# Attention loop: the last query tile projected at heads 33 to 38 instead of 24 to 31, the longest row's selection rounds spread to head 45

## The chip, the cores and the metric

The kernel runs on one core of a Trainium2 chip. The metric is the device time of one execution in microseconds (us). Five engines work beside each other, each through its own instruction list in order: TensorE (PE, with PEld for its weight loads), VectorE (DVE), ScalarE (ACT), GpSimd (POOL) and SyncE (SP). They wait for each other only where an instruction list has a wait on a semaphore.

## The reference, cut to what matters

Two decoder layers over 512 tokens of width 1024. Each layer projects its modulated input into the queries, keys and values of two head groups; group A is attention over a window of 128 tokens with a sink, group B attends only to the 128 keys that an indexer picks for each query:

```python
def one_block(args):                    # 128 queries of group B
    rel = jax.nn.relu(jnp.einsum('bqhd,bsd->bqhs', qib, ki).astype(jnp.float32))
    score = jnp.einsum('bqhs,bqh->bqs', rel, wb)
    score = jnp.where(causal[None], score, -jnp.inf)
    _, sel = lax.top_k(score, topk)     # topk = 128
    ...
    s = jnp.einsum('bqhgd,bqnhd->bqhgn', qg, ks).astype(jnp.float32) * (D ** -0.5)
    p = jax.nn.softmax(s, axis=-1).astype(v.dtype)
    o = jnp.einsum('bqhgn,bqnhd->bqhgd', p, vs)
```

Both outputs are rms-normalised, joined and projected; layer norm, a SwiGLU block and a second layer norm follow.

## The kernel before

Tokens come in four tiles of 128 (t = 0 to 3). All large products are made three times, on high and low parts of both operands (`split_product`, lines 846 to 848), because the operands are rounded. Weights come in pieces of 128x1024 through a ring of four; each is split into a high half by ACT (line 1628) and a low half by DVE, or by POOL for the first output pieces (line 682).

The attention of a layer is one loop of 64 heads, in eight units of eight: A0, A1, A2, A3 (heads 0 to 31), then B0, B1, B3, B2 (heads 32 to 63). Every engine has its own loop over the same index i, and steps are placed in it by lags and tables of indices. At index i

- PE computes the scores of head i (line 1170; from head 48 on two heads at a time, line 1146), transposes the probabilities of head i-3 (line 1181) and multiplies those of head i-5 by the values (line 1203). The scores wait until DVE has masked head i-2, or i-3 where three banks rotate (from `QB_FREE` on); the transposes wait for ACT's exponential. After each unit its output is transposed (line 1211), and DVE and ACT split it.
- DVE adds the mask and takes the maximum (`mask_scores`, line 2288). ACT takes the exponential (line 1718) and copies the transposed probabilities (line 1727). Behind each unit DVE normalises (lines 2314 to 2321), ACT squares (1737), POOL takes the root (646), ACT scales (1744), and the high and low halves of the transposed output follow (ACT 1751, DVE 2338).

Two more jobs ride in the same loop. The first is the projection of group B's queries, four tiles of four steps. A step (`project_qb`) is one weight piece on one tile: two `split_product`, six matmuls of 128x512 into bank 5. `QB_STEPS` gives the head index of every step; the first three run ahead of the loop. When a tile is done, ACT copies it out (line 1667, one index later), POOL rotates it (lines 576, 577, 582, at `ROPE_AT`, two indices later), PE transposes it (line 1106, at `QB_AT`) and ACT copies the transposes (1694). Tile 3 is needed by unit B3, from head 48 on. Bank 5 is also used to reduce a modulation vector in the first layer (line 868, at `REDUCE_AT`; DVE takes it two indices later, line 2148) and, from head `QB_FREE` on, as a third bank for scores.

The second is the indexer's choice of 128 keys. Sixteen rounds on each of three rows (t = 3: 512 wide, t = 2: 384, t = 1: 256) each take the eight largest (`top_max`, line 2241) and strike them out (`top_replace`, line 2249). Two rounds of each row come ahead of the loop, three more of the longest; `ROUNDS_AT` places the others. `top_mask` (line 2266) then turns a row into a mask, at `MASKS_AT`; it is needed by the first head of its unit. In DVE's loop a head's maxima stand ahead of its mask and the replacements behind it.

On POOL, `GAIN_AT` places the scaling of the output weights (line 674) and `WO_AT` their low halves.

Of the kernel before, what the change touches and what calls it, by code (L numbers as in the profile page):

```python
# [20 lines left out]
TOPK = min(256, SEQ // 4)  # L21
# [5 lines left out]
T = SEQ // P  # L27
# [10 lines left out]
CP = tuple(KD // k for k in CK)  # L38
# [25 lines left out]
def own_units(n):  # L64

    units = [("G1", 0), ("X", 0)]
    for f in range(n):
# [15 lines left out]
P_RING = 4  # L83
QB_BANK = 5

QB_FREE = 40
REDUCE_AT = 36
PAIRS_FROM = 48
PT_RING = 4
DVE_HEADS = (3, 7)  # L90
# [3 lines left out]


QB_FRONT = 3
QB_STEPS = (None,) * QB_FRONT + (1,) + tuple(4 + 5 * n // 2 for n in range((T - 1) * CP[4]))
ROPE_AT = tuple(QB_STEPS[CP[4] * t + CP[4] - 1] + 2 for t in range(T))
QB_AT = (9, 21, 30, 45)

# [8 lines left out]
EARLY_ROUNDS = 2  # L109
INDEX_ROUNDS = 3  # L110
ROUNDS_AT = {1: [5 * n // 2 for n in range(TOPK // 8 - EARLY_ROUNDS)],
             2: [8, 12, 16, 19, 24, 26, 29] + [39, 41, 43, 46, 48, 50, 52],
             3: [1 + 13 * n // 4 for n in range(TOPK // 8 - EARLY_ROUNDS - INDEX_ROUNDS)]}
ROUND_TILES = {i: [t for t in IDX_TILES if i in ROUNDS_AT[t]] for i in range(64)}
MASKS_AT = {36: (1,), 41: (3,), 54: (2,)}


SH1, SC1, SH2, SC2, GT1, GT2 = range(6)
# [19 lines left out]
def build_trunk(nc, x, x_t, c_col, positions, inv_freq, weights, w_ada, b_ada, b_gate, ln_col, ln_row, sinks, g_col, out):  # L138
    with ExitStack() as ctx:
# [311 lines left out]
        def at_evac(l, c, t):  # L451

            return at_chunk(l, c, t) - T
# [4 lines left out]
        def at_head(l, u, h):  # L458
            return 64 * l + 8 * u + h + 1
# [76 lines left out]
        def s_bank(n):  # L536

            return bank[3 + n % 2] if n < QB_FREE else bank[(QB_BANK, 3, 4)[(n - QB_FREE) % 3]]

# [296 lines left out]
        def _(pe):  # L836
# [312 lines left out]
            def head_scores(l, u, h):  # L1149
# [7 lines left out]
                else:  # L1157

                    pe.wait_ge(masked, at_head(l, u, h) - (2 if n < QB_FREE else 3))
                if n == QB_FREE:  # L1160
                    pe.wait_ge(proj_evac, at_evac(l, 4, T - 1))
# [11 lines left out]
            def transpose_p(l, u, h):  # L1173
                lo, hi = keys_of(UNITS[u])
                pe.wait_ge(probs, at_head(l, u, h))
                if before := back(u, h, 2):

                    wait_pT(pe, l, *before)
                n = 8 * u + h
                for b in range((hi - lo) // P):  # L1180
                    m = pe.transpose(bank[6 + h % 2][:, b * P:(b + 1) * P],  # L1181
                                     prob[:, n % P_RING, b * P:(b + 1) * P], ident[:])
                m.then_inc(p_transposed, 1)
# [74 lines left out]
            def attention(l):  # L1258
                in_bank2 = ("chunk", 3)
                for i in range(64 + LAG_Y):  # L1260
                    if i == REDUCE_AT and l == 0:

# [6 lines left out]
                    if 0 <= i - LAG_T < 64:  # L1269
                        transpose_p(l, (i - LAG_T) // 8, (i - LAG_T) % 8)  # L1270
                    if i in QB_STEPS:
                        project_qb(l, QB_STEPS.index(i) // CP[4], QB_STEPS.index(i) % CP[4])
                    if 0 <= i - LAG_V < 64:
# [341 lines left out]
        def _(act):  # L1615
# [114 lines left out]
            def sink_weight(l, u):  # L1730
                act.wait_ge(sink_diff, 4 * l + u + 1)
                nc.scalar.activation(es[:, u % 2, :], es[:, u % 2, :], ACT.Exp).then_inc(sink_exp, 1)
# [21 lines left out]
            def attention(l):  # L1754
                for i in range(64 + LAG_SPLIT):
# [4 lines left out]
                    if i < 64:  # L1760
                        exponential(l, i // 8, i % 8)
                        u, h = i // 8, i % 8
                        if h == 7 and UNITS[u][0] == "A":
                            sink_weight(l, u)
                    if i - 1 in QB_STEPS[CP[4] - 1::CP[4]]:
                        evacuate(l, 4, QB_STEPS.index(i - 1) // CP[4])
                    for lag, part in ((LAG_NORM, square_y), (LAG_SCALE, scale_y), (LAG_SPLIT, split_y)):
# [303 lines left out]
        def _(dve):  # L2071
# [405 lines left out]
            def attention(l):  # L2477
                for i in range(64 + LAG_SPLIT):
                    for t in ROUND_TILES.get(i, ()):
                        top_max(t)  # L2480
                    if i == REDUCE_AT + 2 and l == 0:
                        take_mod(2, QB_BANK)
# [5 lines left out]
                    for t in ROUND_TILES.get(i, ()):  # L2488
                        top_replace(t)
                    for t in MASKS_AT.get(i, ()):  # L2490
                        top_mask(t)
# [515 lines left out]
```

## Time and profile before

| | |
|---|---|
| median of 3 runs | 1244.72 us (1244.66 to 1244.84) |
| profiled execution | 1244.9 us, span from first to last instruction 1243.2 us, granted TensorE clock 0.998 |
| PE busy | 1208.3 us (97% of the span) |
| DVE, ACT, POOL busy | 945.8, 594.5, 359.7 us (76%, 48%, 29%) |
| attention loop, first layer | heads 0 to 63 from 125.9 to about 229.5 us |
| attention loop, second layer | from about 735 to 836.6 us |

The profile names an instruction by line, engine, operation and the tiles it writes and reads. "Busy" is the time in which an engine had an instruction at work; an entry in square brackets is the idle time ahead of an instruction and what ended it. PE's and DVE's instructions overlap a little at their ends, so the distance between two starts is what one costs in a row of them.

### The profile page before, as it was taken

The page shows a single profiled execution, that of the slowest core. Times are in us where ns is not written, and L with a number is a line of the kernel's source. Part 1 is how long each engine was busy: PE and PEld are TensorE (multiplying, and loading weights), DVE is VectorE, ACT ScalarE, POOL GpSimd, SP SyncE. Part 2 cuts the span into 40 slices and gives each one's busy share as a digit, 9 for nine tenths or more (in the row PEclk, how much of TensorE's full clock was granted, in tenths as well). Part 3 has the DMA queues.
Part 4 walks back from the last instruction along what each step waited for, and adds up shares of the span by engine and source line. Part 5 has one row for each costly group of instructions (what it writes and reads, how often), then busy time and mean ns, then how long its engine had stood idle before and what let it go on. Part 6 is the DMA issues. An engine that isn't in the chain of part 4 may idle for free. (4 is left out here: it accounts for less than half of the span.)

```text
span 1243.2 us, 20784 instructions
## 1 busy us (share of the span) xinstructions
PE 1208.3 (97%) x7354; PEld 1056.4 (85%) x7354; DVE 945.8 (76%) x1634; ACT 594.5 (48%) x1206; POOL 359.7 (29%) x345
## 2 busy tenths in 40 slices
PE   6999999999999999999999999999999999999997
PEld 5778887889888889999888688778989998899986
DVE  6899987777788795777876599858796776377648
ACT  3655668345333233555144566871545552255520
POOL 4237337600121001221117367581012200122200
PEclk9999999999999999999999999999999999999999
DMA  9872201434888422334833220114223333133331
GB/s 357 323 267 88 86 15 55 135 119 138 279 283 268 148 85 85 105 112 150 296 91 113 69 69 2 35 52 170 85 77 98 115 119 104 60 115 110 119 107 68
DMA packets 45452, 160.75 MB, mean 129 GB/s; under 512 B 5936, under 2 KB 5936, under 8 KB 45360
## 3 DMA queue, kind: packets, MB, share of 16 engines
q1 hardware_dynamic: 30528, 109.07, 26.9%
q0 software_dynamic: 13536, 49.29, 11.7%
q10 hardware_dynamic: 1296, 1.17, 0.3%
q8 instruction: 57, 0.93, 0.3%
q14 instruction: 35, 0.29, 0.1%
HBM read 157.41 MB, written 2.10 MB: 128 GB/s over the span
## 5 line engine op out<-in xcount | busy, mean ns | idle before, releaser
L1628 ACT ACTIVATE w_hi<-w_raw 128x1024 fp32r<-128x1024 f32 x104 | 108.4, 1060 | 152.5 <-PE bank L848 140.2
L846 PE MATMUL bank<-w_hi,hT_hi 128*128 128x512 f32 (+2 forms) x392 | 148.1, 378 | 3.5 <-ACT pq L1667 2.0
L2090 DVE TENSOR_TENSOR w_lo<-w_raw,w_hi 128x1024 fp32r<-128x1024 f32 x96 | 123.7, 1303 | 28.4 <-ACT w_hi L1628 27.0
L848 PE MATMUL bank<-w_hi,hT_lo 128*128 128x512 f32 (+2 forms) x392 | 142.6, 364 | 0.0
L847 PE MATMUL bank<-w_lo,hT_hi 128*128 128x512 f32 (+2 forms) x392 | 142.5, 363 | 0.0
L715 POOL TENSOR_TENSOR w_raw<-ada_w,w_raw 128x512 f32<-128x512 f32 x28 | 37.1, 1325 | 363.2 <-DVE w_lo L2648 200.7
L1312 PE MATMUL bank<-hT_lo,w_hi 128*128 128x256 f32 x448 | 112.3, 283 | 0.0
L1310 PE MATMUL bank<-hT_hi,w_hi 128*128 128x256 f32 x448 | 112.3, 283 | 0.0
L846 PE MATMUL bank<-w_hi,gu_hi 128*128 128x512 f32 x264 | 102.9, 390 | 0.0
L848 PE MATMUL bank<-w_hi,gu_lo 128*128 128x512 f32 x264 | 102.7, 389 | 0.0
L847 PE MATMUL bank<-w_lo,gu_hi 128*128 128x512 f32 x264 | 102.7, 389 | 0.0
L846 PEld LDWEIGHTS bank<-w_hi,hT_hi 128*128 128x128 f32 x392 | 73.9, 188 | 22.4 <-issue 7.0
L1312 PEld LDWEIGHTS bank<-hT_lo,w_hi 128*128 128x128 f32 x448 | 86.0, 192 | 0.1
L1310 PEld LDWEIGHTS bank<-hT_hi,w_hi 128*128 128x128 f32 x448 | 86.0, 192 | 0.1
L2655 DVE TENSOR_TENSOR w_lo<-w_raw,w_hi 128x1024 fp32r<-128x1024 f32 x28 | 34.3, 1225 | 65.2 <-POOL ada_w L720 54.8
L848 PEld LDWEIGHTS bank<-w_hi,hT_lo 128*128 128x128 f32 x392 | 73.9, 188 | 11.6
L847 PEld LDWEIGHTS bank<-w_lo,hT_hi 128*128 128x128 f32 x392 | 74.0, 189 | 9.9 <-issue 0.5
L1718 ACT ACTIVATE pq<-pq,nmax 128x256 f32<-128x256 f32 (+3 forms) x128 | 66.7, 521 | 30.4 <-DVE nmax L2288 29.8
L646 POOL TENSOR_TENSOR rs_out<-rs_in,minus_half 128x1 f32<-128x1 f32 x31 | 21.4, 690 | 201.8 <-DVE rs_in L2365 160.7
L846 PE MATMUL bank<-hT_hi,w_hi 128*128 128x512 f32 x192 | 75.1, 391 | 0.0
L848 PE MATMUL bank<-hT_hi,w_lo 128*128 128x512 f32 x192 | 74.8, 389 | 0.0
L847 PE MATMUL bank<-hT_lo,w_hi 128*128 128x512 f32 x192 | 74.7, 389 | 0.0
(308 smaller groups left out, 3266.7 us busy)
## 6 DMA issues: line engine op xcount, KB each, us to landing
w_raw<-in_weights SPq DMA_DIRECT2D x184, 512.0 KB, 3.6
ada_w<-in_w_ada POOLq DMA_DIRECT2D x76, 512.0 KB, 5.3
ada_w<-in_w_ada SPq DMA_DIRECT2D x4, 512.0 KB, 6.7
qT<-in_w_ada SPq DMA_DIRECT2D x4, 512.0 KB, 10.3
xs<-in_x_t SPq DMA_DIRECT2D x4, 512.0 KB, 16.3
xs<-in_x POOLq DMA_DIRECT2D x4, 512.0 KB, 6.8
g_row<-in_ln_row POOLq DMA_DIRECT2D x4, 512.0 KB, 6.0
b_row<-in_ln_row POOLq DMA_DIRECT2D x4, 512.0 KB, 6.9
```

The source lines that it names most:

```text
L646: nc.gpsimd.tensor_tensor(rs_out[:, n:n + 1], rs_in[:, n:n + 1], minus_half[:], ALU.pow)\
L715: nc.gpsimd.tensor_tensor(gate[:, 0:HALF], x_row[:, HALF:PW], gate[:, 0:HALF], ALU.subtract)\
L846: pe.matmul(dst, a_hi, b_hi, start=first, stop=False)
L847: pe.matmul(dst, a_hi, b_lo, start=False, stop=False)
L848: return pe.matmul(dst, a_lo, b_hi, start=False, stop=last)
L1310: pe.matmul(dst, w, m_hi[:, k, :], start=first and k == 0, stop=False, skip_group_check=not first)
L1312: pe.matmul(dst, w, m_lo[:, k, :], start=False, stop=False, skip_group_check=not first)
L1628: nc.scalar.activation(w_hi[:, p % RING, :], w_raw[:, p % RING, :], ACT.Copy).then_inc(hi_ready, 1)
L1718: nc.scalar.activation(p, p, ACT.Exp, scale=-1.0, bias=nmax[:, u % 2, h:h + 1], accum_out=rowsum[:, u % 2, h:h + 1]).then_inc(probs, 1)
L2090: nc.vector.tensor_tensor(w_lo[:, p % RING, :], w_raw[:, p % RING, :], w_hi[:, p % RING, :].bitcast(F32), ALU.subtract).then_inc(lo_ready, 1)
L2655: nc.vector.tensor_tensor(both_in(w_lo, r, "S2", f), w_raw[:, slot(r.l, gate_piece(r, f)), :], both_in(w_hi, r, "S2", f).bitcast(F32), ALU ...
```

## The change

Two single indices and three tables of indices change, and a new table names the steps of the last tile. No instruction is added or taken away; where rows differ in number, neighbours are counted together differently.

```diff
-QB_FREE = 40
-REDUCE_AT = 36
+QB_FREE = 44
+REDUCE_AT = 41
@@
-QB_STEPS = (None,) * QB_FRONT + (1,) + tuple(4 + 5 * n // 2 for n in range((T - 1) * CP[4]))
+QB_LAST = (33, 35, 37, 38)
+QB_STEPS = (None,) * QB_FRONT + (1,) + tuple(4 + 5 * n // 2 for n in range((T - 2) * CP[4])) + QB_LAST
@@
-             3: [1 + 13 * n // 4 for n in range(TOPK // 8 - EARLY_ROUNDS - INDEX_ROUNDS)]}
+             3: [1 + 22 * n // 5 for n in range(TOPK // 8 - EARLY_ROUNDS - INDEX_ROUNDS)]}
@@
-MASKS_AT = {36: (1,), 41: (3,), 54: (2,)}
+MASKS_AT = {36: (1,), 46: (3,), 54: (2,)}
```

The steps of tile 3 were at heads 24, 26, 29 and 31 and are at 33, 35, 37 and 38. Through `ROPE_AT`, POOL's rotation of tile 3 goes from index 33 to 40. The eleven rounds of the 512-wide row were at heads 1, 4, 7, 10, 14, 17, 20, 23, 27, 30, 33 and are at 1, 5, 9, 14, 18, 23, 27, 31, 36, 40, 45. Since a line is added near the top, every line number behind it is one higher in the changed kernel.

PE at head 33, the second head of unit B0 (scores, transposes of head 30, values of head 28, scores of head 34), before:

```order
L1170 MATMUL bank4<-kT,qT 128x128
L1181 MATMUL bank6<-ident,pq 128x128 x2
L1203 MATMUL bank1<-v_a,pT 128x128 x2
L1170 MATMUL bank3<-kT,qT 128x128
L1181 MATMUL bank7<-ident,pq 128x128 x2
```

and in the changed kernel:

```order
L1171 MATMUL bank4<-kT,qT 128x128
L1182 MATMUL bank6<-ident,pq 128x128 x2
L847 MATMUL bank5<-w_hi,hT_hi 128x512
L848 MATMUL bank5<-w_lo,hT_hi 128x512
L849 MATMUL bank5<-w_hi,hT_lo 128x512
L847 MATMUL bank5<-w_hi,hT_hi 128x512
L848 MATMUL bank5<-w_lo,hT_hi 128x512
L849 MATMUL bank5<-w_hi,hT_lo 128x512
L1204 MATMUL bank1<-v_a,pT 128x128 x2
```

The six matmuls of one projection step have come between the transposes and the values; they stood in the same place of head 24.

DVE at heads 40 and 41, the first of unit B1 (`ISA pq,nmax` is the masked maximum), before:

```order
L2288 ISA pq,nmax<-bank5,scores 128x256
L2288 ISA nmax 128x1
L2241 MAX top8<-scores 128x8
L2288 ISA pq,nmax<-bank3,scores 128x256
L2288 ISA nmax 128x1
L2249 MATCH_REPLACE scores<-top8,scores 128x384
L2266 TENSOR_SCALAR scores<-scores 128x512
```

and in the changed kernel:

```order
L2242 MAX top8<-scores 128x8
L2289 ISA pq,nmax<-bank3,scores 128x256
L2289 ISA nmax 128x1
L2250 MATCH_REPLACE scores<-top8,scores 128x512
L2242 MAX top8<-scores 128x8
L2289 ISA pq,nmax<-bank4,scores 128x256
L2289 ISA nmax 128x1
L2250 MATCH_REPLACE scores<-top8,scores 128x384
```

A round of the 512-wide row now surrounds the mask of head 40, the row's `top_mask` (line 2266) has gone from here, and the scores of these two heads come in banks 3 and 4.

POOL from the root of unit 2 on, before:

```order
L646 TENSOR_TENSOR rs_out<-rs_in,minus_half 128x1
L576 TENSOR_TENSOR scratch<-pq,sin_t 128x512
L577 TENSOR_TENSOR scratch<-pq,cos_t 128x512
L582 TENSOR_TENSOR pq<-scratch 128x512
L795 DMA scratch<-in_b_gate 128x1024
L646 TENSOR_TENSOR rs_out<-rs_in,minus_half 128x1
L674 TENSOR_SCALAR w_raw<-w_raw,gcol 128x512 x2
L682 TENSOR_TENSOR w_lo<-w_raw,w_hi 128x1024
```

and in the changed kernel:

```order
L647 TENSOR_TENSOR rs_out<-rs_in,minus_half 128x1 x2
L675 TENSOR_SCALAR w_raw<-w_raw,gcol 128x512 x2
L577 TENSOR_TENSOR scratch<-pq,sin_t 128x512
L578 TENSOR_TENSOR scratch<-pq,cos_t 128x512
L583 TENSOR_TENSOR pq<-scratch 128x512
L796 DMA scratch<-in_b_gate 128x1024
L683 TENSOR_TENSOR w_lo<-w_raw,w_hi 128x1024
```

The rotation of tile 3 and the DMA of the gate row behind it have moved from ahead of the root of unit 3 and the first gain to behind them.

## Rows read from the trace of the kernel before

**Rows 1.** Windows: start:end, length, busy (x instructions) of each engine, clock, DMA.

```profile
core 0: us, PE busy (x) PEld busy (x) DVE busy (x) ACT busy (x) POOL busy (x), PEclk, DMA share, GB/s
161.06:177.03 15.97, 15.50 (x99) 13.34 (x98) 14.58 (x52) 10.89 (x36) 4.74 (x5) 1.00 0.01 2
177.03:196.47 19.44, 17.49 (x134) 15.39 (x133) 14.69 (x62) 15.99 (x57) 13.02 (x11) 1.00 0.15 43
...
784.58:803.59 19.01, 16.01 (x119) 13.69 (x117) 14.96 (x61) 15.82 (x57) 13.03 (x11) 1.00 0.13 43
```

**Rows 2.** PE in time, head 24: start, duration, instruction, [idle ahead, its releaser].

```profile
162.35 0.50 PE L846 MATMUL bank<-w_hi,hT_hi 128*128 128x512 f32 x1 [0.47 <-ACT pq L1667]
...
164.28 0.60 PE L1170 MATMUL bank<-kT,qT 128*128 128x256 f32 x2
```

**Rows 3.** DVE in time, first layer, start of head 24 and heads 28 to 30.

```profile
162.77 0.55 DVE L2241 MAX8 top<-scores 128x8 f32<-128x384 f32 x1
...
171.20 0.48 DVE L2288 CUSTOM_DVE_ANT_0 pq<-bank,band,nsink 128x256 f32<-128x256 f32 x1
...
171.60 0.56 DVE L2241 MAX8 top<-scores 128x8 f32<-128x384 f32 x1
172.07 0.47 DVE L2288 CUSTOM_DVE_ANT_0 pq<-bank,band,nsink 128x256 f32<-128x256 f32 x1
...
173.00 0.16 DVE L2314 TENSOR_TENSOR es<-rowsum,es 128x8 f32<-128x8 f32 x1
...
174.04 1.01 DVE L2241 MAX8 top<-scores 128x8 f32<-128x512 f32 x2
174.97 0.47 DVE L2288 CUSTOM_DVE_ANT_0 pq<-bank,band,nsink 128x256 f32<-128x256 f32 x1
...
176.42 0.15 DVE L2330 TENSOR_SCALAR rs_in<-mean_sq 128x1 f32<-128x1 f32 x1
```

**Rows 4.** PE in time, first layer: heads 33, the reduction, 39 and 48.

```profile
177.91 0.39 PE L1170 MATMUL bank<-kT,qT 128*128 128x128 f32 x2
...
180.91 1.84 PE L868 MATMUL bank<-ones,ada_acc 128*128 128x1 f32 x16
...
184.58 0.39 PE L1170 MATMUL bank<-kT,qT 128*128 128x128 f32 x2
...
196.47 1.13 PE L1146 MATMUL bank<-kT,qT 64*128 64x512 f32 x4
```

**Rows 5.** PE in time, second layer: head 38, transposes of head 45, scores of 48.

```profile
790.40 0.49 PE L1170 MATMUL bank<-kT,qT 128*128 128x128 f32 x2 [0.44 <-DVE nmax L2288]
...
800.76 0.63 PE L1106 MATMUL bank<-ident,pq 128*128 128x128 f32 x4 [0.84 <-DVE hT_lo L2338]
...
803.59 1.13 PE L1146 MATMUL bank<-kT,qT 64*128 64x512 f32 x4
```

**Rows 6.** DVE and ACT in time: mask of head 42 in both layers, normalisation, square.

```profile
189.52 0.42 DVE L2288 CUSTOM_DVE_ANT_0 pq<-bank,scores 128x256 f32<-128x256 f32 x1
...
796.63 0.42 DVE L2288 CUSTOM_DVE_ANT_0 pq<-bank,scores 128x256 f32<-128x256 f32 x1
...
801.45 0.69 DVE L2321 TENSOR_TENSOR pk<-bank,recip 128x512 f32<-128x512 f32 x1
...
802.25 0.59 ACT L1737 ACTIVATE bank<-pk 128x512 f32<-128x512 f32 x1
```

**Rows 7.** POOL and DVE in time, first layer: rotation, gain, low half, two column masks.

```profile
179.53 1.28 POOL L576 TENSOR_TENSOR scratch<-pq,sin_t 128x512 f32<-128x512 f32 x1 [2.33 <-ACT pq L1667]
...
186.93 3.12 POOL L674 TENSOR_SCALAR w_raw<-w_raw,gcol 128x512 f32<-128x512 f32 x2
...
207.74 2.36 POOL L682 TENSOR_TENSOR w_lo<-w_raw,w_hi 128x1024 fp32r<-128x1024 f32 x1 [2.71 <-ACT w_hi L1628]
...
189.07 0.41 DVE L2266 TENSOR_SCALAR scores<-scores 128x512 f32<-128x512 f32 x1
...
208.29 2.02 DVE L2266 TENSOR_SCALAR scores<-scores 128x384 f32<-128x384 f32 x1
```

## The prediction, made before the changed kernel was run

> **What bounds the kernel now.** A new order of the same work can only win where TensorE (PE) idles, so I read the busy times of the attention loop first, the only part that is reordered (64 heads in each layer) [rows 1]. Heads 24 to 31 last 15.97 us; PE is busy in 15.50 and VectorE (DVE) in 14.58, so PE sets the pace and DVE is close behind. Heads 32 to 47 last 19.44 us in the first layer and 19.01 in the second, with PE busy in 17.49 and 16.01: some 2 and 3 us of bubbles. That, with a wait at head 24, is the whole prize. The order of time of PE then says where the bubbles of the second layer lie: from head 38 on, 0.44 us for DVE's masked scores at head 38, 0.84 for DVE's low half ahead of the transposes of the last query tile [rows 5]. The scores of head 48 come at 196.47 and 803.59 us [rows 4, 5]; from there PE is nearly always busy, so what shifts them shifts the end.
>
> All steps below are on the first layer's clock. Head 32 starts 607.55 us later in the second layer (784.58 against 177.03 [rows 1]), and I subtract that.
>
> **Part 1: four projection blocks leave heads 24 to 31.** Head 24 lasts from 161.06 [rows 1] to 164.28 [rows 2], 3.22 us; a head without a block takes 1.10. A block of six products adds about 1.40, and 0.72 is the wait for ACT's (ScalarE's) copy of the tile before, shown as 0.47 idle [rows 2]. So 4 x 1.40 + 0.72 = 6.3 us leave, and PE alone would need 9.65 us for the eight heads.
>
> DVE does not let it, because the scores of head n wait until the mask of head n-2 is done. DVE's steps, start to start [rows 3]: a 256-wide mask 0.40; a selection round on the 384-wide row 0.47 for the maximum and 0.53 for the replacement, 1.00 together; the 512 and 256 rows together 0.93 + 1.05, which I split by length into 1.26 and 0.73; the normalisation 1.04. In heads 24 to 31 the new order has 8 masks (3.2), 3 rounds of 256 (2.2), 3 of 384 (3.0), still 2 of 512 (2.5; heads 27 and 31 for 27 and 30), the normalisation, a low half of 0.6 with 0.2 of wait, and 0.3 of small ones: 13.0 us. DVE starts head 24 at 162.77 [rows 3]; with the round of head 20 gone I take 162.25, not the whole 1.26 earlier, since it then waits for scores. So head 31 is through at 175.3, and its mask, for which head 33 waits, is done at 174.45. Head 33 started at 177.91 [rows 4]. **Of 6.3 us removed, 3.4 arrive at head 33**; the rest becomes PE idle, in heads 29 to 33.
>
> **Part 2: the blocks come back at heads 33, 35, 37 and 38.** They cost 4 x 1.40 = 5.6 us on PE, on the path, since there was no bubble before head 38. They replace the wait of head 38 in the second layer (0.44), and in the first the reduction of 1.84 us [rows 4], which moves from head 36 to 41. With the intervals of before plus the blocks, from 174.45: head 38 at 183.0, head 39 at 185.0. Before, head 38 of the second layer was at 182.85 [rows 5], head 39 of the first at 184.58 [rows 4].
>
> **Part 3: heads 39 to 47, where DVE and ACT set the pace.** The change puts two 512 rounds here (heads 40 and 45), and the PE blocks are over by then. DVE cannot use the slow heads 33 to 38 to get ahead, since it waits for their scores. From head 39 on: mask at 185.5, round done 186.25; head 40 with the 512 row and a 0.34 mask until 187.85; head 41 until 189.2; the mask of head 42 ends at 189.55. Before, it ended at 189.87 in the first layer and 189.43 in the second [rows 6]. From there to the scores of head 48 the chain was 6.6 us in both layers ([rows 4, 5] less those two): exponential, ACT's conversion of a weight piece, high half, low half, masks, normalisation, ACT's square, ACT's copy of the queries. The 512 round of head 45 falls into it. ACT's square began at 802.25, 0.2 after the product of the normalisation (801.45, 0.6 to the next) was there [rows 6]; apart from that the round adds to the chain, 1.15 us.
>
> Second layer: 189.55 + 6.6 + 1.15 = 197.3 against 196.04, **+1.3 us**.
>
> First layer: the reduction now stands ahead of the scores of head 41 and waits for ACT's copy of the last tile, which follows the exponential of head 39. It starts at about 186.8 and ends at 188.6; DVE gets the scores of head 41 some 0.9 late, and head 42 is masked at 190.4. 190.4 + 6.6 + 1.15 = 198.15 against 196.47, **+1.7 us**.
>
> **GpSimd (POOL).** The rotation of the last query tile, three operations of 1.28 us [rows 7], moves behind the root of unit 3 and the gain of 3.12. Asked for at 184.7, the root, gain and rotation end at 192.5; the transposes of head 45 wait for DVE's low half until 193.1 or later. That cover is 0.6 us. Behind the rotation are queued the gate row's DMA, the low half of the first output piece, the next gain and the root of unit 4, which ends at about 199.5; ACT wants it at 198.7 in the second layer, ahead of a conversion and the copy on which PE waits at head 50. I take **+0.2 us**. SyncE's piece loads hang on POOL's low halves; no PE wait of the loop is for them, and a slip of 2 us is no longer than the head shift.
>
> **Parts at nothing.** The 512-wide column mask moves from head 41 to 46, 0.41 us either way. Two score banks instead of three for heads 40 to 43: DVE's pace hides it; uncovered, a few tenths. The two 512 rounds that leave heads 0 to 23 gave DVE's time only, where PE set the pace.
>
> **The sum**: 1.3 + 1.7 + 0.2 = +3.2 us. The profiled execution took 1244.9 us (span 1243.2, 1.7 around it), the median of the runs is 1244.72; so **1247.9 us**.
>
> **Rivals.**
> - *The bubbles are filled.* PE runs without a gap through heads 33 to 47, DVE and ACT having caught up. By busy times: 17.49 + 5.6 - 19.44 - 3.4 = +0.25 in the first layer, 16.01 + 5.6 - 19.01 - 3.4 = -0.8 in the second: 1244.2. For it: the room in [rows 1]. Against: the blocks end at head 38, where the bubbles begin. 20%.
> - *Faster.* DVE keeps up in heads 24 to 31 as well; all 6.3 us arrive, up to 2 x 2.9 less than the last case, 1238.4, and 1241.3 with half. It decides once DVE does those heads in under 11.5 us. Against it: the 13.0 above is DVE's own work. 7%.
> - *POOL last.* If root, gain and rotation slip by more than the 0.6 us of cover, or ACT waits longer for the root of unit 4, each further microsecond counts: about 1 us in each layer, 1250. 8%.
> - *The column mask of head 46 meets POOL.* The 384-wide one took 2.02 us and ended 0.2 after POOL's low half of 207.74; the 512-wide one took 0.41 although POOL was in its gain from 186.93 on [rows 7]. At head 46, about 197.2, the gain runs (195.8 to 198.9), so I take no wait; were the low half there, 1.5 us a layer, 1250.9. 5%. The Trainium skill (SBUF — State Buffer, "SBUF: two separate sides") has an exclusive lock there, with the second to start waiting for any GpSimd operation. By that page the gain would hold the mask too; the 0.41 speaks against it.
> - *The forecast*, +1.5 to +4.5: 60%.
>
> **Chances.** About 0.2%, 2.5 us, is what a measurement of this kernel tells from no change, and the forecast lies just past it. Slower by more: 0.42 of the forecast's 0.60, with POOL's 0.08 and the mask's 0.05, 0.55. Within: 0.18 and the filled bubbles' 0.20, 0.38. Faster: 0.07. The range, from just under the filled bubbles to the mask case: 1243.6 to 1250.9.
>
> **What would show it.** Right: heads 24 to 31 about 12.5 to 13 us long, with PE waiting for DVE's masks for some 3 us; no PE idle in heads 34 to 38; the gaps of heads 40 to 47 still there and wider; the scores of head 48 1.3 and 1.7 us later in their layers; heads 48 on unchanged at 33.0 us. Wrong: heads 24 to 31 at 10 us (DVE was not close), heads 40 to 47 without gaps (a lead did carry), or PE waiting for POOL's rotation at head 45.

## The result and the profile after

The changed kernel takes **1251.31 us** (median of six runs, 1250.95 to 1251.48) against 1244.74 us for the kernel before in the same session: a ratio of 1.0051, 95% interval 1.0040 to 1.0062. It is slower by 6.6 us. The profiled execution spans 1249.4 us against 1243.2. The direction was forecast, the size was not: +3.2 us was, and the measured time lies 0.4 us above the end of the range.

The loop of 64 heads can be cut where its scores start. This table holds the lengths of five stretches in us, first layer / second layer, from the starts of the score matmuls in PE's order of time. From head 48 on PE computes the scores of two heads at a time, so head 60 is the seventh of these pairs:

| stretch | before | changed | difference | forecast |
|---|---|---|---|---|
| head 0 to 24 | 35.17 / 34.94 | 35.16 / 34.94 | 0.0 / 0.0 | 0 |
| head 24 to 33 | 16.85 / 16.87 | 14.21 / 14.21 | -2.64 / -2.66 | -3.46 |
| head 33 to 39 | 6.67 / 5.99 | 10.54 / 10.53 | +3.87 / +4.54 | +3.88 / +4.56 |
| head 39 to 48 | 11.89 / 12.13 | 13.33 / 12.24 | +1.44 / +0.11 | +1.26 / +0.17 |
| head 48 to 60 | 21.48 / 21.48 | 21.87 / 22.41 | +0.39 / +0.93 | +0.2 once |

That is +3.05 and +2.92 us. Another +0.28 stands ahead of head 0 of the first layer, where nothing was changed; in the other kernels below this offset lies between -0.20 and +0.50, so I count it to no edit. The three make 6.25 us, and the span grew by 6.2. The 0.4 us between that and the 6.6 of the medians is in no trace: the profiled execution was 0.2 us above its median before and 0.2 below it in the changed kernel.

The busy times of the same stretches up to head 48, as in [rows 1], of the changed kernel (start:end, length, busy time of each engine, clock, DMA):

```profile
core 0: us, PE busy (x) PEld busy (x) DVE busy (x) ACT busy (x) POOL busy (x), PEclk, DMA share, GB/s
161.33:175.54 14.21, 11.82 (x82) 10.05 (x80) 13.98 (x49) 9.64 (x33) 4.35 (x5) 1.00 0.01 2
175.54:186.08 10.54, 10.54 (x69) 9.50 (x70) 6.92 (x30) 7.27 (x29) 0.30 (x1) 1.00 0.00 1
186.08:199.41 13.33, 11.19 (x83) 9.88 (x81) 10.61 (x39) 9.40 (x29) 12.93 (x10) 1.00 0.25 74
...
771.88:786.09 14.21, 11.81 (x82) 10.05 (x81) 13.98 (x49) 9.64 (x33) 9.31 (x9) 1.00 0.01 2
786.09:796.62 10.53, 10.53 (x68) 9.50 (x69) 6.91 (x30) 7.27 (x29) 0.29 (x1) 1.00 0.01 2
796.62:808.86 12.24, 9.85 (x67) 8.03 (x65) 10.35 (x38) 9.29 (x29) 11.84 (x10) 1.00 0.17 52
```

In heads 24 to 32 the two engines have changed places: DVE is busy in 13.98 of 14.21 us and PE in 11.8, where PE was busy in 15.50 of the 15.97 us of heads 24 to 31 before [rows 1]. In heads 33 to 38 PE is busy without a gap and DVE has 3.6 us to spare. What PE waited for in the attention loop of the first layer, in the changed kernel (engine, line, what it waited for: us, times, longest):

```profile
PE bank L1171 <- DVE nmax L2289: 3.1, 6, 0.9
PE bank L1147 <- ACT qT L1695: 1.2, 1, 1.2
PE bank L1107 <- DVE hT_lo L2339: 0.7, 1, 0.7
```

The first line is the masks that PE now waits for, the second the copy of the queries ahead of head 48, where PE did not wait before. In order of time PE's places are these (they answer to [rows 4] and [rows 5]):

```profile
175.54 0.49 PE L1171 MATMUL bank<-kT,qT 128*128 128x128 f32 x2 [0.20 <-DVE nmax L2289]
...
187.86 1.95 PE L869 MATMUL bank<-ones,ada_acc 128*128 128x1 f32 x16 [0.30 <-ACT pq L1668]
...
195.39 0.63 PE L1107 MATMUL bank<-ident,pq 128*128 128x128 f32 x4 [0.65 <-DVE hT_lo L2339]
...
199.41 1.13 PE L1147 MATMUL bank<-kT,qT 64*128 64x512 f32 x4 [1.19 <-ACT qT L1695]
...
808.86 1.13 PE L1147 MATMUL bank<-kT,qT 64*128 64x512 f32 x4 [1.19 <-ACT qT L1695]
```

Two places explain most of what the forecast lacks. The first is at the end of head 23. VectorE's difference of unit 2, on operands of 128x8, takes 1.00 us where it took 0.17, with GpSimd's rotation of the third query tile started 0.3 us ahead of it (DVE, then POOL, in the changed kernel):

```profile
161.75 1.00 DVE L2304 TENSOR_TENSOR es<-nmax,nsink 128x8 f32<-128x8 f32 x1
162.67 0.08 DVE L2250 MATCH_VALUE_LOAD scores<-top,scores 128x8 f32 x1
...
161.45 1.27 POOL L577 TENSOR_TENSOR scratch<-pq,sin_t 128x512 f32<-128x512 f32 x1
```

The difference ends at 162.75, GpSimd's first product at 162.72. The second layer has the same row, 1.00 us at 772.29. Before, the difference came first:

```profile
162.02 0.17 DVE L2303 TENSOR_TENSOR es<-nmax,nsink 128x8 f32<-128x8 f32 x1
...
162.38 1.30 POOL L576 TENSOR_TENSOR scratch<-pq,sin_t 128x512 f32<-128x512 f32 x1 [0.75 <-ACT pq L1667]
```

The second place is GpSimd's order of time in the second layer, from the root of unit 3 on, with the step of ScalarE that waits for its end:

```profile
796.33 0.55 POOL L647 TENSOR_TENSOR rs_out<-rs_in,minus_half 128x1 f32<-128x1 f32 x1 [10.65 <-DVE rs_in L2331]
796.86 3.12 POOL L675 TENSOR_SCALAR w_raw<-w_raw,gcol 128x512 f32<-128x512 f32 x2
799.96 1.27 POOL L577 TENSOR_TENSOR scratch<-pq,sin_t 128x512 f32<-128x512 f32 x1
...
804.76 2.38 POOL L683 TENSOR_TENSOR w_lo<-w_raw,w_hi 128x1024 fp32r<-128x1024 f32 x1
807.12 3.36 POOL L675 TENSOR_SCALAR w_raw<-w_raw,gcol 128x512 f32<-128x512 f32 x2
810.45 0.57 POOL L647 TENSOR_TENSOR rs_out<-rs_in,minus_half 128x1 f32<-128x1 f32 x1
...
811.05 0.72 ACT L1745 ACTIVATE pk<-pk,rs_out 128x512 f32<-128x512 f32 x1 [0.70 <-POOL rs_out L647]
```

After 10.65 us of idle time GpSimd works through 14.7 us without a real gap, and the root of unit 4 is its last piece. ScalarE stands for 0.70 us, with a conversion of 1.04 us and the next heads' copies and exponentials behind the wait.

A smaller third is the column mask of head 46, which now stands beside the scores of head 48. In the first layer it began in the last 0.4 us of GpSimd's gain and took 0.69 us (DVE, then POOL), in the second 0.42 (808.72):

```profile
199.27 0.69 DVE L2267 TENSOR_SCALAR scores<-scores 128x512 f32<-128x512 f32 x1
...
196.57 3.11 POOL L675 TENSOR_SCALAR w_raw<-w_raw,gcol 128x512 f32<-128x512 f32 x2
```

### The profile page after: what moved, and what is told of

It reads as the page before. It is cut to its first block and busy times, and to the rows that moved or that the text cites. A ratio compares the mean times of both kernels' runs of the same rounds, so it can differ in the third digit from the quotient of the medians.

```text
span 1249.4 us, 20787 instructions
## 1 busy us (share of the span) xinstructions
PE 1209.8 (97%) x7354; PEld 1057.9 (85%) x7354; DVE 946.8 (76%) x1634; ACT 595.9 (48%) x1206; POOL 359.9 (29%) x345
## 3 DMA queue, kind: packets, MB, share of 16 engines
q10 hardware_dynamic: 1296, 1.17, 0.3%
```

## The experiments

The table gives the lengths of the stretches for every kernel (first / second layer, us) and the sum of each layer against before; the text below each expectation says what follows. The profiled executions of one kernel and the next agree to 0.1 us wherever nothing was changed, so a few tenths can be read in a stretch though not in a total. Some of the expectations count a pair of heads behind head 48 as one: their "head 51" and "head 54" are heads 54 and 60, and their "root of unit 5" is the root of unit 4, which ScalarE waits for behind head 48.

| kernel | 24 to 33 | 33 to 39 | 39 to 48 | 48 to 60 | layers against before | median us |
|---|---|---|---|---|---|---|
| before | 16.85 / 16.87 | 6.67 / 5.99 | 11.89 / 12.13 | 21.48 / 21.48 | | 1244.7 to 1244.9 |
| changed | 14.21 / 14.21 | 10.54 / 10.53 | 13.33 / 12.24 | 21.87 / 22.41 | +3.05 / +2.92 | 1251.31 |
| rounds only | 16.11 / 16.12 | 6.76 / 6.72 | 14.10 / 14.10 | 21.61 / 21.61 | +1.68 / +2.08 | 1248.49 |
| blocks only | 14.60 / 14.57 | 10.53 / 10.53 | 12.60 / 11.17 | 21.48 / 22.70 | +2.26 / +2.50 | 1250.19 |
| copy late | 13.39 / 13.82 | 10.53 / 10.53 | 13.32 / 12.23 | 21.85 / 22.42 | +2.19 / +2.50 | 1250.02 |
| rounds by 38 | 14.22 / 14.22 | 10.53 / 10.53 | 13.68 / 10.61 | 21.48 / 24.38 | +3.00 / +3.26 | 1251.07 |
| gain first | 14.22 / 14.22 | 10.53 / 10.53 | 14.28 / 12.23 | 21.60 / 21.60 | +3.64 / +2.15 | 1250.26 |
| root before gain | 14.22 / 14.22 | 10.52 / 10.53 | 13.33 / 12.23 | 22.35 / 22.36 | +3.50 / +2.88 | 1251.59 |
| root and round | 14.22 / 14.22 | 10.53 / 10.53 | 13.28 / 11.19 | 22.31 / 22.31 | +3.40 / +1.80 | 1250.01 |
| three mended | 13.39 / 13.81 | 10.52 / 10.52 | 12.28 / 10.41 | 21.48 / 22.62 | +0.72 / +0.88 | 1246.92 |
| four mended | 13.38 / 13.80 | 10.53 / 10.52 | 12.27 / 10.40 | 21.92 / 21.92 | +1.17 / +0.18 | 1246.76 |
| blocks 2 and 2 | 13.79 / 13.87 | 8.44 / 8.84 | 13.35 / 13.35 | 21.48 / 21.49 | +0.06 / +1.06 | 1247.97 |
| blocks 3 and 1 | 14.77 / 14.79 | 6.72 / 6.72 | 15.87 / 15.81 | 21.48 / 21.13 | +1.86 / +2.02 | 1249.30 |
| first block at 25 | 16.26 / 16.24 | 6.67 / 5.59 | 11.89 / 12.01 | 21.49 / 21.49 | -0.66 / -1.14 | 1243.04 |

### Each half of the change alone

Rounds only, an edit of the kernel before:

```diff
-             3: [1 + 13 * n // 4 for n in range(TOPK // 8 - EARLY_ROUNDS - INDEX_ROUNDS)]}
-MASKS_AT = {36: (1,), 41: (3,), 54: (2,)}
+             3: [1 + 22 * n // 5 for n in range(TOPK // 8 - EARLY_ROUNDS - INDEX_ROUNDS)]}
+MASKS_AT = {36: (1,), 46: (3,), 54: (2,)}
```

> The kernel before with the second half of the change alone: the longest row's selection rounds at heads 1, 5, 9, 14, ... 36, 40, 45 and its column mask at head 46; the projection blocks stay at heads 24 to 31. My theory: the 512-wide round of head 45 (a maximum of 0.69 and a replacement of 0.68, 1.2 us start to start) stands on the chain from the mask of head 42 to the scores of head 48, and the root of unit 5 is asked for later by the same step, so ScalarE waits for it ahead of head 50. Head 48 about 1.2 us later in each layer, its wait on ScalarE's copy of the queries there as in the changed kernel (1.19), another 0.3 to 0.9 by head 51: +2.5 to +3.5 us in all, 1247.2 to 1248.2. Rival, the rounds cost only together with the blocks (DVE gets to head 45 late because of them): within 1 us of the kernel before, no wait at head 48.

Measured: 1248.49 us, ratio 1.0029 (1.0019 to 1.0040). The wait of 1.19 us ahead of head 48 is there in both layers, as the theory has it, and the rival falls. Behind head 48 only 0.13 us are lost, less than the 0.3 to 0.9 that I expected, and ScalarE's wait for the root does not show. Heads 39 to 47 cost 2.2 and 2.0 us more, not 1.2, since the round of head 40 is paid here too; heads 24 to 32 give 0.75 back. Head 25 starts 2.49 us after head 24 in the first layer, 3.22 before: the wait of the first block for ScalarE's copy has gone.

Blocks only, the changed kernel with these two lines put back (`13 * n // 4`, mask at 41).

> The changed kernel with the rounds and the column mask of the longest row back where they were (heads 1, 4, 7, ... 30, 33; mask at head 41); the last tile's blocks stay at heads 33, 35, 37, 38 and the reduction at head 41. My theory: heads 24 to 32 as in the changed kernel (14.2 us instead of 16.9), heads 33 to 38 too, then heads 39 to 47 without the two 512-wide rounds: head 48 1.2 to 1.8 us earlier than in the changed kernel in each layer, so +1.2 in the first layer and 0 to +0.5 in the second against before, and no wait for the root of unit 5. In all about +2 us with the collision of the es difference in it (0.8 us a layer): 1246 to 1248. If the two halves add up, this one and the run with the rounds alone together make the 6.6 us of the whole; rival, each half alone costs little (under 1 us) and only both together meet.

Measured: 1250.19 us, ratio 1.0042 (1.0025 to 1.0059), 2.2 us above the top of what I expected. The halves give +3.6 and +5.3 us, together 8.8 against the 6.6 of the whole, so they don't add up. Behind the blocks the two late rounds cost less than in the kernel before: the stretch from head 39 to 48 is 0.7 and 1.1 us longer in the changed kernel than with the blocks alone. And in the second layer blocks only loses 1.22 us after head 48, where I had expected nothing: ScalarE waits 1.11 us for the root of unit 4. The root is ready at 809.92, whatever VectorE has gained by then. The second layer's column mask also met the rotation there, 1.30 us at 799.17.

### The small difference under the rotation

Copy late, an edit of the changed kernel in ScalarE's loop:

```diff
-                    if i - 1 in QB_STEPS[CP[4] - 1::CP[4]]:
-                        evacuate(l, 4, QB_STEPS.index(i - 1) // CP[4])
+                    for t in [t for t in range(T) if i == QB_STEPS[CP[4] * t + CP[4] - 1] + (2 if t == 2 else 1)]:
+                        evacuate(l, 4, t)
```

> The changed kernel with ScalarE's copy of the third query tile one place later, behind the sink weight of head 23, so that GpSimd's rotation of that tile can't begin before VectorE's 128x8 difference of unit 2 is through (1.00 us in the changed kernel, 0.17 in the kernel before). My theory: the difference takes 0.17 again in both layers, and since VectorE sets the pace of heads 24 to 33 the 0.83 arrive at head 33 and at the end: -1.7 us, 1249.6. Rival: the 0.83 are absorbed (PE's idle time at head 26 shrinks, and that of heads 29 to 33 grows): head 33 within 0.2 of the changed kernel, 1251.3.

Measured: 1250.02 us, 1.3 less than the changed kernel. Its rows in DVE's and POOL's order of time, first layer and then second:

```profile
161.90 0.17 DVE L2304 TENSOR_TENSOR es<-nmax,nsink 128x8 f32<-128x8 f32 x1
...
163.16 1.28 POOL L577 TENSOR_TENSOR scratch<-pq,sin_t 128x512 f32<-128x512 f32 x1 [1.66 <-ACT pq L1668]
...
781.23 0.59 DVE L2315 TENSOR_TENSOR es<-rowsum,es 128x8 f32<-128x8 f32 x1
...
779.30 2.50 POOL L697 TENSOR_TENSOR xs<-xs,b_row 128x512 f32<-128x512 f32 x2
```

In the first layer the difference takes 0.17 us, head 33 comes 0.82 sooner, and 0.86 stand at the end: shown. In the second layer the difference takes 0.17 us too, but only 0.4 arrive, so the total falls 0.4 short of the theory. The rotation has moved on to its next collision: GpSimd's row operations behind it now end at 781.80, and VectorE's sum of unit 2, again 128x8, takes 0.59 us until 781.82 (0.15 in the changed kernel).

The Trainium skill (SBUF — State Buffer, "SBUF: two separate sides") has for this that a VectorE instruction with two SBUF inputs and a GpSimd instruction that reads SBUF exclude each other for their whole length. The trace agrees: both stalls end with GpSimd's instruction, within 0.03 us. The prediction cites this section for the column mask and does not apply it to the differences.

### The late rounds, and what stood behind them

Rounds by 38, an edit of the changed kernel:

```diff
-             3: [1 + 22 * n // 5 for n in range(TOPK // 8 - EARLY_ROUNDS - INDEX_ROUNDS)]}
-MASKS_AT = {36: (1,), 46: (3,), 54: (2,)}
+             3: [1, 5, 9, 14, 18, 23, 27, 31, 34, 36, 38]}
+MASKS_AT = {36: (1,), 41: (3,), 54: (2,)}
```

> The changed kernel with the last three rounds of the longest row at heads 34, 36 and 38 instead of 36, 40 and 45, and its column mask at head 41 instead of 46: the same rounds, but in the stretch where PE runs the blocks and VectorE waits for scores (0.85 to 1.05 us idle a head). My theory: nothing is paid at heads 34 to 38; VectorE has 1.2 us less at head 40 and 1.2 less at head 45, so head 48 comes 1.2 to 2 us earlier in each layer, ScalarE's 1.19 wait there is gone, and the wait for the root of unit 5 behind it: -3 to -5 us, 1246.5 to 1248.5. Rival: ScalarE or PE's own work sets heads 39 to 48 and the rounds are beside it: at most -1 us, 1250.3 to 1251.3.

Measured: 1251.07 us, nothing gained: the totals fit the rival, the stretches do not. The rounds of heads 34 and 36 indeed cost nothing (33 to 39 stays 10.53), and in the second layer head 48 comes 1.63 us sooner, without its wait. Then all of it is lost, here on ScalarE and PE:

```profile
811.25 0.72 ACT L1745 ACTIVATE pk<-pk,rs_out 128x512 f32<-128x512 f32 x1 [2.99 <-POOL rs_out L647]
...
813.33 0.41 PE L1182 MATMUL bank<-ident,pq 128*128 128x128 f32 x2 [2.57 <-ACT pT L1728]
```

ScalarE stands for 2.99 us until GpSimd's root, which comes at the same time as in the changed kernel (811.0 there, 811.2 here). So there are two limits one behind the other. GpSimd's rotation is late as well: PE waits 1.09 us for it ahead of the transposes of the last tile (804.30). In the first layer two other things stand where the gain should be. The column mask of head 41 met the rotation (DVE, then POOL), and the granted clock fell:

```profile
191.29 1.35 DVE L2267 TENSOR_SCALAR scores<-scores 128x512 f32<-128x512 f32 x1
...
191.09 1.26 POOL L578 TENSOR_TENSOR scratch<-pq,cos_t 128x512 f32<-128x512 f32 x1
...
190.00:194.00 4.00, 4.00 (x19) 3.45 (x18) 3.47 (x10) 2.01 (x7) 3.69 (x3) 0.61 0.00 0
```

### GpSimd's chain

Gain first, one number in the changed kernel:

```diff
-GAIN_AT = (39, 44, 49, 54, 58, 60, 62, 64)
+GAIN_AT = (37, 44, 49, 54, 58, 60, 62, 64)
```

> The changed kernel with GpSimd's first gain (3.12 us) one place ahead of the root of unit 3 instead of behind it, in the 10.6 us in which GpSimd is idle there in the second layer. The trace of the changed kernel has a chain on GpSimd in the second layer: root of unit 3 at 796.33, gain, rotation of the last tile, the gate row's transfer, low half, second gain, root of unit 4 until 811.0, without a gap; ScalarE waits 0.70 for that root, and in the run with the rounds by head 38 it waits 2.99. My theory: this chain is a second limit just behind that of VectorE; with the gain ahead the whole of it comes 3 us earlier, ScalarE's wait is gone, and head 51 stands 0.7 us earlier in the second layer, 0 to 0.3 in the first: -0.7 to -1.2 us, 1250.1 to 1250.6. Rival: the 0.70 are absorbed by PE's own work in heads 48 to 51: no change, 1251.3.

Measured: 1250.26 us, 1.05 less. In the second layer ScalarE no longer waits for the root, and the stretch behind head 48 is 21.60 us instead of 22.41, nearly the 21.48 of before. That confirms the second limit. The first layer does not answer this question: heads 39 to 48 took 0.95 us more there, most likely because the granted clock was 0.60 from 190 to 192 us and 0.55 from 192 to 194.

Root before gain, the other way to the same end:

```diff
-GAIN_AT = (39, 44, 49, 54, 58, 60, 62, 64)
-WO_AT = (42, 47, 52, 57)
+GAIN_AT = (39, 46, 50, 54, 58, 60, 62, 64)
+WO_AT = (42, 49, 52, 57)
```

> The changed kernel with GpSimd's root of unit 4 ahead of the second gain instead of behind it, and the second low half and its conversion on ScalarE two heads later (49 instead of 47). The heads up to 48 stay as they are. Theory: the stretch from head 48 to head 54, 21.87 and 22.41 us in the changed kernel (first and second layer) against 21.48 in both before, grew because ScalarE waits for that root (0.70 us idle in the second layer) with the probabilities of heads 46 and 47 queued behind the wait; with the root first the stretch is 21.5 again in both layers: -0.4 and -0.9, 1250.0 us. Rival: the growth comes from VectorE (its low half waits 2.40 and 2.96 us for ScalarE's high half there, 2.03 before) and stays, or ScalarE's conversion, now nearer the low half, costs as much at head 52: no change, 1251.3.

Measured: 1251.59 us, no gain: my rival was right. From head 48, head 52 comes 0.65 us sooner in the second layer, but PE then waits 0.63 instead of 0.48 for VectorE's mask at head 54, and the second conversion waits for the gain (0.20) and stands closer to ScalarE's high half. Between heads 54 and 56 another 0.4 us go in both layers. The low half that was moved back pushes GpSimd's third gain back, ScalarE's third conversion waits for that, and PE for the copy behind it (second layer):

```profile
820.31 1.06 ACT L1629 ACTIVATE w_hi<-w_raw 128x1024 fp32r<-128x1024 f32 x1 [0.33 <-POOL w_raw L675]
...
822.00 0.63 PE L1182 MATMUL bank<-ident,pq 128*128 128x128 f32 x4 [0.20 <-ACT pT L1728]
```

The stretch is 22.36 us in the second layer and, worse, 22.35 in the first. The second conversion alone does not hold head 54: in four mended, below, it stands in the same place, no column mask stands at head 46, and head 54 comes 9.37 us after head 48, as before (9.81 here).

Root and round is that kernel with the row's last rounds at heads 36, 38 and 40:

```diff
-             3: [1 + 22 * n // 5 for n in range(TOPK // 8 - EARLY_ROUNDS - INDEX_ROUNDS)]}
+             3: [1, 5, 9, 14, 18, 23, 27, 31, 36, 38, 40]}
```

> The run with the root ahead of the gain, and the longest row's last three rounds at heads 36, 38 and 40 instead of 36, 40 and 45; its column mask stays at head 46. Against that run it prices one 512-wide round on the chain ahead of head 48, with GpSimd's limit out of the way. Theory: head 48 comes 1.0 to 1.2 us sooner in each layer (the prediction's 1.15), ScalarE's 1.19 us wait there is gone, and the gain stays to the end: -2.0 to -2.4 us against the run before it. Rival: the round stood beside the wait for ScalarE's low and high halves: under 0.5 us a layer, -1 us or less in all.

Measured: 1250.01 us, 1.6 less than the run before it and 0.4 short of the theory. The scores of head 48 in the second layer, of root before gain and of this one:

```profile
809.37 1.13 PE L1147 MATMUL bank<-kT,qT 64*128 64x512 f32 x4 [1.19 <-ACT qT L1695]
```

```profile
807.82 1.13 PE L1147 MATMUL bank<-kT,qT 64*128 64x512 f32 x4
```

From head 39 to 48 the second layer takes 11.19 us instead of 12.23, and the 1.04 us last to head 60. That is the price of the round of head 45; the prediction had 1.15. In the first layer 13.28 us stand against 13.33: the granted clock was 0.66 from 190 to 195 us, which most likely hides it.

### All of it mended, and other places for the blocks

Three mended joins copy late, gain first and the rounds by head 38, with the column mask at head 39.

```diff
-GAIN_AT = (39, 44, 49, 54, 58, 60, 62, 64)
+GAIN_AT = (37, 44, 49, 54, 58, 60, 62, 64)
-MASKS_AT = {36: (1,), 46: (3,), 54: (2,)}
+MASKS_AT = {36: (1,), 39: (3,), 54: (2,)}
```

> The changed kernel with three things mended at once: ScalarE's copy of the third tile behind the sink weight (as in the run with the late copy), the last rounds of the longest row at heads 34, 36 and 38 with its mask at head 39 (ahead of GpSimd's rotation, which made that mask 1.35 us instead of 0.41 in the first layer), and the first gain ahead of the root of unit 3. My theory: 0.8 a layer from the copy, 0.9 to 1.6 at head 48 from the rounds, and from head 48 to the end 33.0 us as in the kernel before, since the root of unit 4 is no longer late. Head 48 at 70.3 to 71 us from head 0 in the first layer and 69.3 to 69.8 in the second: about the kernel before, 1244 to 1246. It would show that the whole loss was three collisions and not the blocks. Rival: the blocks in heads 33 to 38 cost in themselves (nothing of DVE's or ACT's idle time there comes back): at least +2 us stay, 1247 or more.

Measured: 1246.92 us, ratio 1.0018 (1.0009 to 1.0028), so 4.4 of the 6.6 us are back. Head 48 stands at 69.67 us from head 0 in the second layer, 0.26 ahead of before; in the first at 71.30, 0.3 beyond what I expected. The second layer then gives 1.14 away behind head 48: ScalarE waits 1.03 for the root again, since VectorE has moved ahead of GpSimd once more.

Four mended adds the order of root before gain to it (`GAIN_AT = (37, 46, 50, ...`, `WO_AT = (42, 49, ...`).

> The run with three things mended, with the root of unit 4 ahead of the second gain as well. There ScalarE waited 1.03 us for that root in the second layer and head 48 to 54 took 22.62 us against 21.48 before. Theory: that stretch is 21.5 again: -1.1 us in the second layer, nothing in the first (21.48 already), so about 1 us above the kernel before in all, 1245.5 to 1246. The blocks in heads 33 to 38 would then cost under 1 us, and the rest of the loss was what stood around them. Rival: another limit takes the root's place (VectorE's masks of 512): no change, 1246.9.

Measured: 1246.76 us, ratio 1.0015 (1.0006 to 1.0024): in the second layer 0.70 less and only 0.18 above before, in the first 0.45 more. The 0.45 are those between heads 54 and 56 again: ScalarE's third conversion waits 0.34 us for the gain in both layers. The total fits the rival, the second layer the theory but for 0.4.

Blocks 2 and 2, and blocks 3 and 1, edits of three mended:

```diff
-QB_LAST = (33, 35, 37, 38)
+QB_LAST = (27, 30, 34, 37)
```

> The run with three things mended, and the last tile's blocks at heads 27, 30, 34 and 37 instead of 33, 35, 37 and 38. In the changed kernel PE idles 2.2 to 2.6 us in heads 24 to 32, where VectorE sets the pace, and PE sets the pace in heads 33 to 38. My theory: two blocks of 1.40 stand in the idle time of heads 24 to 32 for nothing or nearly so, and two are gone from the path: -1.5 to -2.8 us a layer against the run with four blocks behind, so below the kernel before by 1 to 4 us: 1241 to 1244. Rival: a block delays the scores that VectorE waits for next, so PE's and VectorE's times add up rather than overlap: within 1 us of the run with three things mended.

Measured: 1247.97 us (1245.81 to 1248.62), no faster than three mended. Its ten executions fall apart: three took 1245.8 to 1245.9 us, seven 1247.6 to 1248.6, at a mean granted clock of 0.995 to 0.998. The profiled one is of the first kind, so the stretches tell of 1245.9 us, 1 us below three mended's trace; what the others lose, and where, no trace shows. Two blocks among heads 24 to 32 cost only 0.40 and 0.06 us: there my theory holds. The two that are gone from heads 33 to 38 give 2.1 and 1.7 us back. But heads 39 to 47 grow by 1.1 and 2.9, with PE waiting 0.28 and 1.02 us for masks at heads 39 and 40: VectorE has the rounds of heads 36 and 38 and the column mask (1.06 us under the rotation at 794.88) to do and no PE blocks to do them beside.

> As the run with two blocks in each stretch, but with the blocks at heads 26, 29, 31 and 36. By busy times PE would have 9.65 + 4.2 = 13.9 us of work in heads 24 to 32 and VectorE 10.5 to 12.2, so PE sets the pace there again and the third block is paid there instead of behind. My theory: within 0.7 us of the run with the blocks two and two, on either side. Rival, if the copy of the last tile and GpSimd's chain behind it still set heads 44 to 48: 1 to 3 us faster than that run, since the copy comes sooner.

Here `QB_LAST` is (26, 29, 31, 36). Measured: 1249.30 us, 1.3 above the two and two, where I had allowed 0.7. The third block costs 1.0 us in heads 24 to 32, as the busy times said. The rest lies in heads 39 to 47: with the last block at head 36 the rotation falls ahead of the root of unit 3, ScalarE waits 3.04 us for that in both layers, and the granted clock fell in both. How much each costs was not separated (second layer: ACT, PE, and the windows of that place):

```profile
798.58 0.72 ACT L1745 ACTIVATE pk<-pk,rs_out 128x512 f32<-128x512 f32 x1 [3.04 <-POOL rs_out L647]
...
799.61 0.30 PE L1182 MATMUL bank<-ident,pq 128*128 128x128 f32 x1 [2.51 <-ACT pT L1728]
...
796.00:800.00 4.00, 1.19 (x7) 0.72 (x7) 2.49 (x10) 1.42 (x5) 2.22 (x3) 1.00 0.33 114
800.00:804.00 4.00, 4.00 (x20) 3.39 (x19) 1.48 (x5) 3.75 (x12) 1.66 (x1) 0.59 0.06 19
```

### A version that beats both

First block at 25, an edit of the kernel before and nothing else. It puts the first two blocks of the last tile one head later each, at heads 25 and 27:

```diff
-QB_STEPS = (None,) * QB_FRONT + (1,) + tuple(4 + 5 * n // 2 for n in range((T - 1) * CP[4]))
+QB_STEPS = (None,) * QB_FRONT + (1,) + tuple(4 + 5 * n // 2 for n in range((T - 2) * CP[4])) + (25, 27, 29, 31)
```

> The kernel before with the four blocks of the last tile at heads 25, 27, 29 and 31 instead of 24, 26, 29 and 31; nothing else moves. In the kernel before the first block waits at head 24 for ScalarE's copy of the tile before it (0.47 us idle, 0.72 over the plain head), and in the run with the rounds alone moved that wait was gone and heads 24 to 32 took 16.1 us instead of 16.9. Theory: with the block one head later the copy is there, and PE, which sets the pace in these heads, gains 0.5 to 0.7 us a layer: -1.0 to -1.4 us, 1243.3 to 1243.7, a small gain over the kernel before. Rival: VectorE, busy for 14.6 of these 16 us, becomes the limit at heads 26 to 31 and the gain is under 0.2 us a layer: within 0.4 us of the kernel before.

Measured: **1243.04 us** (1242.90 to 1243.44), ratio 0.9986 (0.9977 to 0.9995): 1.8 us below the kernel before, a bit more than expected, and 8.3 below the changed one. The stretch from head 24 to 33:

```profile
160.83:177.09 16.26, 16.26 (x106) 14.10 (x105) 15.32 (x57) 12.58 (x41) 4.92 (x5) 1.00 0.01 2
767.77:784.01 16.24, 16.24 (x107) 14.12 (x105) 15.30 (x57) 12.56 (x40) 9.93 (x9) 1.00 0.01 2
```

PE has no gap left here, 0.6 us a layer gained. In the second layer another 0.5 comes between heads 33 and 48, where PE's second wait for a mask, at head 39 (0.24 us), is gone. There the 256-wide column mask had stood under GpSimd's last product of the rotation (before, and this kernel):

```profile
790.26 0.81 DVE L2266 TENSOR_SCALAR scores<-scores 128x256 f32<-128x256 f32 x1
...
788.80 0.30 DVE L2266 TENSOR_SCALAR scores<-scores 128x256 f32<-128x256 f32 x1
```

## Why the prediction was right in direction and wrong in size

**Right:**
- *Part 1's mechanism.* Heads 24 to 31 last 12.76 us (12.5 to 13 forecast), with VectorE as the limit and 2.4 us of waits for its masks up to head 33 (about 3 forecast).
- *Part 2.* Head 33 to 39 takes 10.54 and 10.53 us, with PE busy throughout; 10.55 was forecast.
- *Part 3.* Head 39 to 48 takes 13.33 and 12.24 us, against 13.15 and 12.3. The reduction starts 1.78 us after head 39 (1.8 forecast). The round of head 45 costs 1.04 (1.15).
- *The filled bubbles* did not come: PE is busy in 11.19 of 13.33 us and 9.85 of 12.24 there.

**Wrong:**
- *Part 1, the start of VectorE's sum.* "With the round of head 20 gone I take 162.25": the first maximum of head 24 came at 163.34. Of the 1.1 us, 0.27 is the offset ahead of the loop and 0.83 the difference held by the rotation. The 13.0 us of work behind it were right, so the whole slip arrived: -2.64 instead of -3.46, in both layers, 1.6 us in all. I had counted what VectorE does and not where GpSimd would then be. Before, the difference starts at 162.02 and the rotation at 162.38, 0.36 us behind it. In the changed kernel the difference is 0.27 us sooner, ScalarE's copy 0.91 (160.80 instead of 161.71), and so the rotation stands ahead: 0.17 us became 1.00. Copy late shows it, 0.86 us in the first layer, and in the second 0.4 because another small sum takes its turn.
- *POOL's +0.2 us and "heads 48 on unchanged".* From head 48 to 60 the layers grew by 0.39 and 0.93 us, 1.1 more than I gave them. The mechanism was written down (the root behind the second gain, ScalarE waiting ahead of a conversion), and as a rival with about 1 us a layer and a chance of 8%. I had the root end at 199.5 where ScalarE wants it at 198.7 in the second layer, and still took 0.2 for these 0.8 us, as if PE had that much to spare. In fact the wait was 0.70 and arrived. The whole chain hangs on the root of unit 3, which the change delays by slowing heads 33 to 38. Gain first gives 0.8 of the second layer's 0.93 back.
- *The column mask at nothing.* "0.41 us either way" is wrong at head 46, from where VectorE carries it to PE's wait for a mask at head 54 (0.47 us in the first layer, 0.20 before). The stretch from head 48 to 60 is 21.48 us where neither that mask nor a wait for the root stands (first layer of blocks only, rounds by 38 and three mended), 21.60 or 21.61 where the mask takes 0.42 (rounds only, gain first), 21.85 and 21.87 where it takes 0.66 and 0.69 (first layer of copy late and of the changed kernel). So the mask is the first layer's 0.39, and the 0.12 of the second that gain first leaves.
- The last 0.28 us is the offset that belongs to no edit.

So 1.6 + 1.1 + 0.3 is 3.0 of the 3.1 us between +3.2 and the 6.25 of the span. The column mask's own rival came in small: 0.27 us in the first layer instead of 1.5 in each, since it met the end of the gain and not the low half. The same mask took 1.35, 1.30 and 1.06 us in kernels where it met GpSimd's products.

As for the change itself: the blocks can stand in heads 33 to 38 for little. With what stood around them mended, the second layer is within 0.2 us of before and the first 1.2 above. But in none of the eleven orders tried here did moving the blocks out of these heads win anything over the kernel before; that no order could is not shown.

## What to carry to other kernels

Where one engine's lead is used up by the next, add up the other engines' chains to the end as well, each from the event that it really starts from: here a repair on VectorE of 1.6 us gave nothing until GpSimd's chain was shortened too. When a change moves two engines against each other in time, list the short operations that used to pass between the long ones. And before moving a whole group of work, try to move only its first members past the wait that they meet: two blocks one head later each won 1.8 us, the whole group seven to nine heads later lost 6.6.

## What the runs showed of the hardware

- A VectorE operation on 128x8 elements with both inputs in SBUF took 1.00 us instead of 0.17 while a GpSimd product of 128x512 ran, and 0.59 instead of 0.15 in another kernel; it ended with GpSimd's instruction each time. Such a wait shows as a longer instruction and not as idle time at a semaphore; the opening of this text, where engines wait only at semaphores, leaves it out.
- A column mask (one input, 128x512) took 0.41 us beside GpSimd's gain (one input) in the kernel before [rows 7] and 1.35 us beside its product of two inputs (rounds by 38). Beside the end of the gain it took 0.69 us in the changed kernel, so the kind of GpSimd's instruction alone does not decide it; what does is open.
- The granted clock fell in four of the profiled executions; at its lower level, 1.2 of 2.4 GHz, windows of 2 us show 0.50. In rounds by 38, gain first and root and round that lasted some 3 us, from about 190 us on, behind the reduction, whose 16 products have one column each. In blocks 3 and 1 it lasted longer in the first layer (0.57, 0.50, 0.50 and 0.72 in the windows of 2 us from 186 to 194), starting while the reduction ran (185.08 to 187.40), and came once more in the second, after 4 us in which PE was busy for 1.19. The changed kernel and six others hold the same reduction at head 41 and kept 1.00 in the profiled execution, so what decides it is open.
